# Two transformer blocks in float32: low parts of the feed-forwards' weight chunks by accumulating DMAs

## The chip, the cores and the metric

One core of a Trainium2 chip runs the whole program. The metric is the device time in microseconds of one execution; for the kernel before the median of three runs is given.

## What is computed

Two blocks of two layers each, on 512 tokens of width 1024, in float32. Every layer holds attention and mixing parts and feed-forwards, six in all:

```python
def swiglu(h, w_gate, w_up, w_down):
    return (jax.nn.silu(h @ w_gate) * (h @ w_up)) @ w_down

x = x + 0.5 * swiglu(rms_norm(x, ffn1_norm[l]), ffn1_w_gate[l], ffn1_w_up[l], ffn1_w_down[l])
...
x = x + 0.5 * swiglu(rms_norm(x, ffn2_norm[l]), ffn2_w_gate[l], ffn2_w_up[l], ffn2_w_down[l])
...
h = h + (jax.nn.silu(u @ w_gate[l]) * (u @ w_up[l])) @ w_down[l]
```

The weights are 1024 x 2816 (gate, up) and 2816 x 1024 (down). First block: feed-forward, mixing (convolutions and sparse attention), cross-attention, feed-forward. Second block: retention and differential attention, feed-forward. A norm ends each block.

## The kernel before

Tokens lie on the free axis: x is eight tiles of 128 x 512, and a product of the weights' chunk `c` (128 output channels, up to eight parts of 128 x 128) with the tokens fills one PSUM bank. A product in full precision is three products of rounded numbers: every operand is a high part, rounded to float32r, and a low part, the rest. `chunk` (L524) issues per part `w_hi * u_hi`, `w_hi * u_lo`, `w_lo * u_hi` (L542 to L544).

A weight chunk goes through a ring of four slots:

- SP's `load` (L431) waits until the low part of the chunk four back is made (`split`), then loads 512 KB into `raw`.
- ScalarE's `round_weights` (L1075) waits for the landing and for TensorE's end of the chunk four back (`tiles`), then writes `w_hi` (L1080).
- VectorE's `rest_of_weights` (L1534) waits for `rounded`, then writes `w_lo = raw - w_hi` (L1537) and counts `split`.
- TensorE's `chunk` waits for `split`.

So `step(p)` on ScalarE and `rest_of_weights(p)` on VectorE, called when chunk p is through TensorE, prepare chunk p + 4. A feed-forward has 68 chunks in three groups (`F_GROUPS`): gate and up chunks in turn (16, 16 and 12), after each eight down chunks of 8, 8 and 6 parts. The second gate and up of every four is mostly a *fast pair* (`fast_pair`, L588): seven half-size products in place of eight. It needs four sums of the pair's raw halves, which GpSimd makes one round ahead (`fast_sums`, L2279 to L2282, semaphore `s_made`); ScalarE rounds them (`sum_hi`, L1123) and VectorE splits them (`sum_lo`, L1601, `s_split`). There are 57 such pairs, seven in the first feed-forward and ten in the others.

At a feed-forward's end VectorE adds each down product to x (L1627), ScalarE and VectorE split the next input (`u_hi` L1084, `u_lo` L1541), and GpSimd's `squares` sums x squared (L2230, L2231). After the first chunk of the next stage (between the two blocks after the third) TensorE's `stat` needs the last square, VectorE scales it (L1577), GpSimd takes the power (L2257). Between the blocks GpSimd also sums a joint norm's squares (L2246).

All queues run in the order in which they are written; waits are on semaphores.

Of the kernel before, what the change touches and what calls it, by code (L numbers as in the profile page):

```python
# [36 lines left out]
KT = D // P  # L37
# [83 lines left out]
L2_AT = [2 * N_L1, 2 * N_L1 + N_L2]  # L121
assert all((n + c) % RING < 3 for n in L2_AT for c in D_V + R_V)

# [47 lines left out]
class At:  # L171


    def __init__(self, base, i=0):
        self.base, self.i = base, i
        self.slot, self.no, self.turn = base % RING, base + 4 * i, base // RING + i
# [5 lines left out]
def swapped(n, c):  # L182

    return c if (n - c % 2) % RING < 3 else c ^ 1

# [23 lines left out]
def two_blocks(nc, A, out):  # L209
    ctx = ExitStack()  # L210
    with ctx:
# [169 lines left out]
        split = sem("split")  # L381
        tiles = sem("tiles")
# [42 lines left out]

        block = ctx.enter_context(nc.Block())
# [94 lines left out]
        def _(pe):  # L521
            mm = nc.tensor.matmul

            def chunk(p, rhs_hi, rhs_lo, kn=KT, last=None, n=S, ks=None, order=None, to=None, after=None):  # L524


                order = order or range(kn)
                ks = ks or order
                if ks[0] == order[0]:
                    pe.wait_ge(split, p.no + RING + 1)  # L530
                    if after is None:
                        pe.wait_ge(taken, p.no + 1)
# [12 lines left out]
                if ks[-1] == order[-1]:  # L545
                    ins.then_inc(tiles, 1)
# [41 lines left out]
            def fast_pair(p, m, fast):  # L588
# [19 lines left out]
                pe.wait_ge(split, p.no + RING + 1)  # L608
# [9 lines left out]
                pe.wait_ge(split, p1.no + RING + 1)  # L618
# [66 lines left out]
            def values(p, hi, lo, blocks, outs, last, n=S, after=None):  # L685

                if blocks[0] == 0:
                    pe.wait_ge(split, p.no + RING + 2)
                    if after is None:
                        pe.wait_ge(taken, p.no + 2)  # L690
                if after is not None:
                    pe.wait_ge(taken, after + RING + 1)
                for t, o in zip(blocks, outs):
                    for k in range(KT):
                        u = slice(k * n + t * P, k * n + (t + 1) * P)
                        mm(o, hi[:, u], two_slots(w_hi, p, k), start=k == 0, stop=False)  # L696
                        mm(o, hi[:, u], two_slots(w_lo, p, k), start=False, stop=False)  # L697
                        ins = mm(o, lo[:, u], two_slots(w_hi, p, k), start=False, stop=k == KT - 1)  # L698
                    if t == last:
                        ins.then_inc(tiles, 2)  # L700
                    elif t == 1:
                        ins.then_inc(v_mm, 1)
# [368 lines left out]
        def _(act):  # L1071
# [3 lines left out]
            def round_weights(p, ahead=RING):  # L1075
# [14 lines left out]
            def step(p, more=True):  # L1090
                if more:
                    round_weights(p)
# [11 lines left out]
            def ffn(n, q, f, gain, more=True, joint=False):  # L1104
                for g, (f0, fn) in enumerate(F_GROUPS):
                    fast = quick(q, g)

                    def pair(p, f_at, h_at):

                        step(p)  # L1110
                        act.wait_ge(taken, p.no + RING + 1)
                        a(tanh_t, gate_t, ACT.Tanh, scale=0.5).then_inc(f_tanh, 1)
                        step(p.plus(1))
                        act.wait_ge(f_prod, F_TILES * f + f_at + 1)
                        a(tile(h_hi, h_at), gate_t, ACT.Copy).then_inc(f_rounded, 1)

                    def fast_pairs(p, m, f_at, h_at):
# [6 lines left out]
                        step(p)  # L1124
                        act.wait_ge(taken, p.no + RING + 1)
                        a(tanh_t, gate_t, ACT.Tanh, scale=0.5).then_inc(f_tanh, 1)
                        step(p.plus(1))
                        act.wait_ge(f_prod, F_TILES * f + f_at + 1)
                        a(tile(h_hi, h_at), gate_t, ACT.Copy).then_inc(f_rounded, 1)
                        step(q2)  # L1130
# [4 lines left out]
                        step(q3)  # L1135
# [3 lines left out]
                    if g == 0:  # L1139
                        if q:  # L1140
                            step(At(n))
                        step(At(n + 1))
# [25 lines left out]
                    def down(p, k, more):  # L1168
                        step(p, more)
# [8 lines left out]
                    if end and not more:  # L1178
                        for k in range(KT):
                            step(At(n + k), k < 4)  # L1180
# [59 lines left out]
            step(At(0))  # L1240
# [289 lines left out]
        def _(v):  # L1530
# [103 lines left out]
            def ffn(n, q, f, gain, factor, more=True):  # L1634

                for g, (f0, fn) in enumerate(F_GROUPS):
# [8 lines left out]
                    def up(p, f_at, h_at):  # L1645
# [6 lines left out]
                        rest_of_weights(p)  # L1652
# [13 lines left out]
                    def fast_up(p, m, f_at, h_at):  # L1666
# [11 lines left out]
                        rest_of_weights(p)  # L1678
# [3 lines left out]
                    if g == 0:  # L1682
                        rest_of_weights(At(n))
# [11 lines left out]
                        rest_of_weights(At(n + 2))  # L1695
# [4 lines left out]
                    with chain.loop(v, 1 if g == 0 else 0, fn // 2, 2 if fast is None else 5) as i:  # L1700
                        if fast is None:
                            for jj in range(2):
                                rest_of_weights(At(n + 2 * jj, i))
                                gate(At(n + 2 * jj, i), i * 2 + (f0 + jj))
                                up(At(n + 2 * jj + 1, i), i * 2 + (f0 + jj), i * 2 + jj)
                        else:
# [3 lines left out]
                            rest_of_weights(At(n, i))  # L1710
                            up(At(n + 1, i), i * 2 + f0, i * 2)
                            rest_of_weights(At(n + 2, i))
# [4 lines left out]
                    if end and not more:  # L1717
                        for k in range(KT):
                            residual(At(n + k), k, factor)
                            if k < 4:  # L1720
                                rest_of_weights(At(n + k))
# [9 lines left out]
                    with out_turns(v, after if end or not after else None) as turn:  # L1731
                        for i in (turn if (end or not after) and after in FAST else [turn]):
                            for j in range(4):
# [3 lines left out]
                                rest_of_weights(At(n + j, i))  # L1737
# [486 lines left out]
        def _(pool):  # L2224
# [11 lines left out]
            def squares(n, q):  # L2236
# [3 lines left out]
                if q == 8:  # L2240
                    chain.done(pool, nc.gpsimd.memset(j_sum, 0.0))
                with chain.loop(pool, 0, 2, 8 if q == 8 else 4) as i:
                    for j in range(4):
                        if q == 8:
                            pool.wait_ge(j_squared, i * 4 + (j + 1))
                            chain.done(pool, tt(j_sum, j_sum, tile(j_sq, i * 4 + j), ALU.add))  # L2246
# [12 lines left out]
            def fast_sums(n, q):  # L2259

                fast = FAST[q]
                pool.wait_ge(stat_diag, q + 1)

                def part(j):
                    return w_sum[:, j * HC:(j + 1) * HC]

                for g, (f0, fn) in enumerate(F_GROUPS):
                    if quick(q, g) is None:
                        n = n + 2 * fn + 8
                        continue  # L2270
                    with chain.loop(pool, 1 if g == 0 else 0, fn // 2, 2) as i:
                        p, m = At(n + 2, i), i + (FAST_PAIRS * fast + FAST_AT[g])
                        p1 = p.plus(1)
                        a11, a12 = raw[:, p.slot, 0:HC], raw[:, p.slot, HC:CH]
                        a21, a22 = raw[:, p1.slot, 0:HC], raw[:, p1.slot, HC:CH]
                        pool.wait_ge(s_split, m + 1)
                        pool.wait_ge(raw_in[p.slot], (p.turn + 1) * 16)
                        pool.wait_ge(raw_in[p1.slot], (p1.turn + 1) * 16)
                        tt(part(S3), a11, a21, ALU.add)  # L2279
                        chain.done(pool, tt(part(S1), a21, a22, ALU.add))  # L2280
                        chain.done(pool, tt(part(S2), part(S1), a11, ALU.add))
                        tt(part(S4), part(S2), a12, ALU.add).then_inc(s_made, 1)  # L2282
                    n = n + 2 * fn + 8
# [8 lines left out]
            for l in range(2):  # L2292
                L = L1_AT[l]
                turned = from_slot(L + O_OUT)
                fast_sums(L, 4 * l)
                squares(L + N_FFN - 8, 4 * l + 1)
# [39 lines left out]
                fast_sums(L + O_FFN2, 4 * l + 3)  # L2336
                squares(L + O_FFN2 + N_FFN - 8, 4 * l + 4)
                norm_inv(4 * l + 4)

            for l in range(2):  # L2340
# [16 lines left out]
                fast_sums(L + O2_FFN, 9 + 2 * l)  # L2357
                if l:
                    n = L + O2_FFN + N_FFN - 8
                    pool.wait_ge(taken, n + RING + 1)  # L2360
                    clear_sum()
                    for k in range(KT - 1):
                        pool.wait_ge(taken, n + k + RING + 1)
                        if k:
                            pool.wait_ge(sq_sum, 8 * 11 + k)
                        add_square(k)
                else:
                    squares(L + O2_FFN + N_FFN - 8, 10)
# [25 lines left out]
```

## Time and profile before

| | |
|---|---|
| median of 3 runs | 3486.97 us (3486.56 to 3487.17) |
| span of the profiled execution | 3487.4 us, 0.4 over that median |
| TensorE busy | 3439.7 us, 99% |
| VectorE | 2422.0 us, 69% |
| ScalarE | 1409.1 us, 40% |
| GpSimd | 958.4 us, 27% |
| loads of weights, share of the 16 DMA engines | 31.4% |

The profiled execution has no time of its own beside its span. A busy share is an average over stages with different limits; which engine a stage hangs on is read from its stretch and its waits. A matmul's busy time is modelled, and matmuls overlap, so TensorE's pace is read from the distance of their starts or of what waits for their ends.

### The profile page before, as it was taken

To read this page: it belongs to the slowest core of one execution; us is meant where nothing else is said; L and a number is where in the kernel's file an instruction comes from. 1 tells how busy PE (TensorE), PEld (TensorE's weight loads), DVE (VectorE), ACT (ScalarE), POOL (GpSimd) and SP (SyncE) were. 2 spreads that over 40 slices of the span, in tenths; PEclk is the share of its full clock that TensorE was granted. 3 is DMA by queue.
4 is the path that set the end of the run, shared out by engine and by line. 5 is a ranking of instruction groups with operands and counts; after the bars stand their busy time and mean duration, and the time that the engine had idled before them with its cause. 6 is when DMAs were issued, how large, how long until landed. Compare 5 with 4: busy or idle time off the path is not lost.

```text
span 3487.4 us, 51264 instructions
## 1 busy us (share of the span) xinstructions
PE 3439.7 (99%) x18454; PEld 2868.7 (82%) x18454; DVE 2422.0 (69%) x3375; ACT 1409.1 (40%) x2163; POOL 958.4 (27%) x631
## 2 busy tenths in 40 slices
PE   8999999999999999999999999999999999999998
PEld 7888786878888888878687888887888888888887
DVE  6667897558567967679755856765696585567755
ACT  4333365344334433336534433434443343443333
POOL 0112394123112511239412311230322130041213
PEclk9999999999999999999999999999999999999999
DMA  5332332323333333243232333331233332223331
GB/s 159 97 99 88 103 103 64 114 82 91 99 100 91 95 104 97 86 107 103 63 114 84 90 98 101 91 91 55 85 96 97 97 96 85 61 73 109 97 97 61
DMA packets 621280, 324.65 MB, mean 93 GB/s; under 512 B 13488, under 2 KB 616520, under 8 KB 621128
## 3 DMA queue, kind: packets, MB, share of 16 engines
q1 hardware_dynamic: 617096, 317.15, 31.4%
q10 hardware_dynamic: 4032, 5.51, 0.6%
q8 instruction: 91, 1.49, 0.2%
q14 instruction: 61, 0.50, 0.0%
HBM read 314.75 MB, written 2.10 MB: 91 GB/s over the span
## 4 chain that ended last, share of the span: by engine, by line
PE 84%; DVE 6%; issue 5%; ACT 2%; POOL 2%; DMA 0%; ACTq 0%; SPq 0%; DVEq 0%; POOLq 0%
PE bank L544 20%; PE bank L542 20%; PE bank L543 20%; PE bank L583 5%; PE bank L585 5%; PE bank L584 5%; POOL mem L2312 1%; PE bank L696 1%; PE bank L697 1%; PE bank L698 1%; DVE w_lo L1537 1%; PE bank L682 1%; PE bank L900 1%; PE bank L884 1%; PE bank L936 1%
## 5 line engine op out<-in xcount | busy, mean ns | idle before, releaser
L1080 ACT ACTIVATE w_hi<-raw 128x1024 fp32r<-128x1024 f32 x602 | 636.0, 1059 | 1201.6 <-PE bank L544 1184.9
L1537 DVE TENSOR_TENSOR w_lo<-raw,w_hi 128x1024 fp32r<-128x1024 f32 x602 | 839.8, 1397 | 202.9 <-ACT w_hi L1080 202.5
L542 PE MATMUL bank<-u_hi,w_hi 128*128 128x512 f32 x1920 | 763.4, 398 | 2.0 <-DVE mem L1546 1.5
L544 PE MATMUL bank<-u_hi,w_lo 128*128 128x512 f32 x1920 | 762.0, 397 | 0.0
L543 PE MATMUL bank<-u_lo,w_hi 128*128 128x512 f32 x1920 | 755.9, 394 | 0.0
L542 PE MATMUL bank<-h_hi,w_hi 128*128 128x512 f32 (+1 forms) x1568 | 606.7, 387 | 2.9 <-DVE h_lo L1541 2.2
L544 PE MATMUL bank<-h_hi,w_lo 128*128 128x512 f32 (+1 forms) x1568 | 608.5, 388 | 0.0
L543 PE MATMUL bank<-h_lo,w_hi 128*128 128x512 f32 (+1 forms) x1568 | 603.3, 385 | 0.0
L2279 POOL TENSOR_TENSOR mem<-raw 128x512 f32<-128x512 f32 x57 | 106.3, 1864 | 1334.4 <-DMA raw<-in_ffn_w_up 570.4
L542 PEld LDWEIGHTS bank<-u_hi,w_hi 128*128 128x128 f32 x1920 | 360.5, 188 | 92.0 <-issue 6.7
L544 PEld LDWEIGHTS bank<-u_hi,w_lo 128*128 128x128 f32 x1920 | 360.4, 188 | 87.1
L543 PEld LDWEIGHTS bank<-u_lo,w_hi 128*128 128x128 f32 x1920 | 360.7, 188 | 85.4
L1627 DVE SCALAR_TENSOR_TENSOR x<-bank,x 128x512 f32 (+1 forms) x192 | 132.4, 689 | 377.9 <-PE bank L544 377.8
L542 PEld LDWEIGHTS bank<-h_hi,w_hi 128*128 128x128 f32 x1568 | 294.4, 188 | 70.1 <-DVE h_lo L1541 4.8
L543 PEld LDWEIGHTS bank<-h_lo,w_hi 128*128 128x128 f32 x1568 | 294.7, 188 | 67.1 <-issue 0.5
L544 PEld LDWEIGHTS bank<-h_hi,w_lo 128*128 128x128 f32 x1568 | 294.5, 188 | 64.1
L2312 POOL TENSOR_TENSOR mem<-mem,spare 128x512 f32<-128x512 f32 x120 | 169.5, 1451 | 106.9 <-ACT spare L1302 106.5
L583 PE MATMUL bank<-t_hi,sum_hi 128*128 128x256 f32 x684 | 190.3, 278 | 3.5 <-DVE sum_lo L1601 3.5
L584 PE MATMUL bank<-t_lo,sum_hi 128*128 128x256 f32 x684 | 189.4, 277 | 0.0
L585 PE MATMUL bank<-t_hi,sum_lo 128*128 128x256 f32 x684 | 189.3, 277 | 0.0
L2231 POOL TENSOR_TENSOR mem<-mem 128x512 f32<-128x512 f32 x95 | 175.8, 1850 | 7.5
L2234 POOL MEMSET mem<- 128x512 f32 x12 | 6.3, 528 | 549.6 <-DVE x L1627 549.6
(300 smaller groups left out, 5863.1 us busy)
## 6 DMA issues: line engine op xcount, KB each, us to landing
raw<-in_w_in SPq DMA_DIRECT2D x96, 512.0 KB, 3.8
raw<-in_ffn_w_gate SPq DMA_DIRECT2D x88, 512.0 KB, 3.8
raw<-in_ffn_w_up SPq DMA_DIRECT2D x88, 512.0 KB, 3.8
raw<-in_ffn_w_down SPq DMA_DIRECT2D x64, 512.0 KB, 3.8
raw<-in_w_gate SPq DMA_DIRECT2D x44, 512.0 KB, 3.8
raw<-in_w_up SPq DMA_DIRECT2D x44, 512.0 KB, 3.8
raw<-in_w_out SPq DMA_DIRECT2D x32, 512.0 KB, 4.1
raw<-in_xa_wkv SPq DMA_DIRECT2D x32, 512.0 KB, 3.9
```

What stands on the lines that cost most here:

```text
L542: mm(o, w_hi[:, s, w], rhs_hi[:, r], start=k == order[0], stop=False)
L543: mm(o, w_hi[:, s, w], rhs_lo[:, r], start=False, stop=False)
L544: ins = mm(o, w_lo[:, s, w], rhs_hi[:, r], start=False, stop=k == order[-1])
L583: mm(o, wh, rh, start=k == 0, stop=False)
L584: mm(o, wh, rl, start=False, stop=False)
L585: ins = mm(o, wl, rh, start=False, stop=k == KT // 2 - 1)
L1080: a(w_hi[:, p.slot, :], raw[:, p.slot, :], ACT.Copy).then_inc(rounded, 1)
L1537: tt(w_lo[:, p.slot, :], raw[:, p.slot, :], f32(w_hi[:, p.slot, :]), ALU.subtract).then_inc(split, 1)
L1627: stt(tile(x, k), bank[p.slot][:, :], factor, tile(x, k), ALU.mult, ALU.add).then_inc(taken, 1)
L2231: tt(sumsq, sumsq, square, ALU.add).then_inc(sq_sum, 1)
L2279: tt(part(S3), a11, a21, ALU.add)
L2312: tt(conv[n % 2], conv[n % 2], tap_t[n % 4], ALU.add).then_inc(tap_added, 1)
```

## The change

In the feed-forwards VectorE no longer makes the chunks' low parts. ScalarE writes two roundings of the raw chunk, `w_hi` and, with a factor of -1, `w_lo`; then a DMA that GpSimd issues adds the raw chunk onto `w_lo`. Its landing is counted per slot (`low_in`), and TensorE and SP wait for that. GpSimd's program in a feed-forward is written out chunk by chunk, with the pairs' sums and the squares between the transfers. The descriptor memory for GpSimd's DMAs grows from 256 to 512 bytes a partition. The first four chunks of the program and all chunks of other stages stay with VectorE.

```diff
+FFN_AT = [0, O_FFN2, N_L1, N_L1 + O_FFN2, L2_AT[0] + O2_FFN, L2_AT[1] + O2_FFN]
+LOW = [c for n in FFN_AT for c in range(n + RING, n + N_FFN + RING) if c < N_ALL]
+def low_count(c):
+    return sum(b <= c and b % RING == c % RING for b in LOW)
...
+        def wait_split(eng, p):
+            if p.base + (0 if isinstance(p.i, int) else RING) in LOW:
+                eng.wait_ge(low_in[p.slot], (low_count(p.base) + p.i) * 16)
+            else:
+                eng.wait_ge(split, p.no + RING + 1 - sum(b < p.base for b in LOW))
...
-                sp_e.wait_ge(split, p.no + 1)
+                if p.base >= RING:
+                    wait_split(sp_e, p.plus(-RING))
...
-                    pe.wait_ge(split, p.no + RING + 1)
+                    wait_split(pe, p)
...
-                a(w_hi[:, p.slot, :], raw[:, p.slot, :], ACT.Copy).then_inc(rounded, 1)
+                ins = a(w_hi[:, p.slot, :], raw[:, p.slot, :], ACT.Copy)
+                if negated:
+                    ins = a(w_lo[:, p.slot, :], raw[:, p.slot, :], ACT.Copy, scale=-1.0)
+                ins.then_inc(rounded, 1)
...
-                        rest_of_weights(p)
                         v.wait_ge(f_rounded, F_TILES * f + f_at + 1)
...
+            def low(c):
+                pool.wait_ge(rounded, c + RING + 1)
+                nc.gpsimd.dma_start(w_lo[:, c % RING, :], raw[:, c % RING, :], accum_op=ALU.add).then_inc(low_in[c % RING], 16)
...
+            def first_sums(c, m):
+                a11, a12, a21, a22 = halves_of(c)
+                pool.wait_ge(s_split, m + 1)
+                for each in (c, c + 1):
+                    pool.wait_ge(raw_in[each % RING], (each // RING + 1) * 16)
+                tt(part(S3), a11, a21, ALU.add)
+                chain.done(pool, tt(part(S1), a21, a22, ALU.add))
+            def second_sums(c, m):
+                a11, a12, a21, a22 = halves_of(c)
+                chain.done(pool, tt(part(S2), part(S1), a11, ALU.add))
+                tt(part(S4), part(S2), a12, ALU.add).then_inc(s_made, 1)
+            def ffn(n, q, to=None):
...
+                        low(c)
...
+                            first_sums(*pairs[0])
+                        low(c + 1)
+                        if ahead:
+                            second_sums(*pairs.pop(0))
+                        low(c + 2)
+                        low(c + 3)
...
+                    for k in range(8):
+                        low(n + k)
+                        if k == 4 and pairs and pairs[0][0] == n + 10:
+                            first_sums(*pairs[0])
+                            second_sums(*pairs.pop(0))
...
+            def squares_and_low(n, q, to):
+                pool.wait_ge(taken, n + RING + 1)
+                clear_sum()
...
+                for k in range(KT):
+                    if not last or k < 4:
+                        low(n + k)
...
+                    add_square(k)
...
-    nc = bacc.Bacc("TRN2", target_bir_lowering=False, num_devices=1, dynamic_dma_scratch_size=256)
+    nc = bacc.Bacc("TRN2", target_bir_lowering=False, num_devices=1, dynamic_dma_scratch_size=512)
```

GpSimd in a round with a fast pair, first feed-forward; `mem` holds the sums. First before (the loop's body), then with the change.

```order
L2277 ISA [waits s_split]
L2279 TENSOR_TENSOR mem<-raw 128x512 [waits raw_in3,raw_in2]
L2280 TENSOR_TENSOR mem<-raw 128x512
L196 ISA
L2281 TENSOR_TENSOR mem<-mem,raw 128x512 [waits chain_p]
L196 REGISTER_ALU
L2282 TENSOR_TENSOR mem<-mem,raw 128x512 [waits chain_p]
```

```order
L2272 DMA w_lo<-raw 128x1024 [waits rounded] x3
L2288 TENSOR_TENSOR mem<-raw 128x512 [waits raw_in3,raw_in2,s_split]
L2289 TENSOR_TENSOR mem<-raw 128x512
L2272 DMA w_lo<-raw 128x1024 [waits rounded,chain_p]
L2294 TENSOR_TENSOR mem<-mem,raw 128x512
L2295 TENSOR_TENSOR mem<-mem,raw 128x512 [waits chain_p]
```

The four sums, alone before, now stand after one transfer and around another, and the next transfers stand behind them.

ScalarE at the start of the same round, before and with the change:

```order
L1122 ISA [waits s_made]
L1123 ACTIVATE sum_hi<-mem 128x2048 [waits w_mm]
L1077 ISA
L1079 REGISTER_ALU [waits raw_in0]
L1080 ACTIVATE w_hi<-raw 128x1024 [waits tiles]
L1125 REGISTER_ALU
L1126 ACTIVATE mem<-mem 128x512 [waits taken]
```

```order
L1147 ISA [waits s_made]
L1148 ACTIVATE sum_hi<-mem 128x2048 [waits w_mm]
L1099 ISA
L1101 REGISTER_ALU [waits raw_in0]
L1102 ACTIVATE w_hi<-raw 128x1024 [waits tiles]
L1104 ACTIVATE w_lo<-raw 128x1024
L1150 REGISTER_ALU
L1151 ACTIVATE mem<-mem 128x512 [waits taken]
```

The second rounding stands ahead of the tanh (L1126, now L1151).

GpSimd in the last down group of a feed-forward, before (`squares`, the first of four in the loop's body) and with the change:

```order
L2234 MEMSET mem 128x512 [waits taken]
L202 UNCONDITIONAL_BRANCH [waits chain_p]
L202 ISA
L2230 ISA [waits taken]
L2230 TENSOR_TENSOR mem<-x 128x512
L196 REGISTER_ALU
L2231 TENSOR_TENSOR mem<-mem 128x512 [waits chain_p]
```

```order
L2249 MEMSET mem 128x512 [waits taken]
L2272 DMA w_lo<-raw 128x1024 [waits rounded,chain_p]
L2245 TENSOR_TENSOR mem<-x 128x512 [waits taken]
L2246 TENSOR_TENSOR mem<-mem 128x512 [waits chain_p]
L2272 DMA w_lo<-raw 128x1024 [waits rounded]
L2245 TENSOR_TENSOR mem<-x 128x512 [waits sq_sum,taken]
```

Each chunk's square and sum now stand behind that chunk's transfer.

## Rows read from the trace of the kernel before

**Rows 1.** The page's first part: the span, and each engine's busy time, share and instructions.

```profile
span 3487.4 us, 51264 instructions
...
PE 3439.7 (99%) x18454; PEld 2868.7 (82%) x18454; DVE 2422.0 (69%) x3375; ACT 1409.1 (40%) x2163; POOL 958.4 (27%) x631
```

**Rows 2.** Busy time by stretch: the second feed-forward of layer 0.

```profile
core 0: us, PE busy (x) PEld busy (x) DVE busy (x) ACT busy (x) POOL busy (x), PEclk, DMA share, GB/s
805.00:1152.00 347.00, 345.77 (x1901) 296.89 (x1900) 256.53 (x284) 131.40 (x149) 90.93 (x55) 1.00 0.33 96
```

**Rows 3.** What TensorE waited for: us in total, times, longest.

```profile
PE bank L583 <- DVE sum_lo L1601: 3.5, 5, 0.9
...
PE bank L542 <- DVE h_lo L1541: 2.2, 6, 0.4
...
PE bank L542 <- DVE w_lo L1537: 0.7, 2, 0.4
```

**Rows 4.** Groups by line: busy, mean ns of one | idle before, releaser.

```profile
L1080 ACT ACTIVATE w_hi<-raw 128x1024 fp32r<-128x1024 f32 x602 | 636.0, 1059 | 1201.6 <-PE bank L544 1184.9
L1537 DVE TENSOR_TENSOR w_lo<-raw,w_hi 128x1024 fp32r<-128x1024 f32 x602 | 839.8, 1397 | 202.9 <-ACT w_hi L1080 202.5
```

**Rows 5.** Timeline (start, us) of ScalarE and SP's queue in a down group.

```profile
1043.90 1.06 ACT L1080 ACTIVATE w_hi<-raw 128x1024 fp32r<-128x1024 f32 x1 [4.54 <-PE bank L544]
1049.50 1.06 ACT L1080 ACTIVATE w_hi<-raw 128x1024 fp32r<-128x1024 f32 x1 [4.54 <-PE bank L544]
...
1046.25 0.37 SPq L436 DMA_DIRECT2D raw<-in_ffn_w_up  x1
```

**Rows 6.** Timeline of a round with a fast pair: ScalarE, then GpSimd.

```profile
1081.72 1.06 ACT L1080 ACTIVATE w_hi<-raw 128x1024 fp32r<-128x1024 f32 x1
...
1102.73 1.06 ACT L1080 ACTIVATE w_hi<-raw 128x1024 fp32r<-128x1024 f32 x1 [0.32 <-PE bank L544]
...
1084.86 2.03 POOL L2279 TENSOR_TENSOR mem<-raw 128x512 f32<-128x512 f32 x1 [14.32 <-DVE sum_lo L1601]
1086.85 1.29 POOL L2280 TENSOR_TENSOR mem<-raw 128x512 f32<-128x512 f32 x1
1088.22 1.63 POOL L2281 TENSOR_TENSOR mem<-mem,raw 128x512 f32<-128x512 f32 x1
1089.92 1.62 POOL L2282 TENSOR_TENSOR mem<-mem,raw 128x512 f32<-128x512 f32 x1
```

**Rows 7.** DMA queues (packets, MB, share); issues (count, KB each, us to landing).

```profile
q1 hardware_dynamic: 617096, 317.15, 31.4%
...
raw<-in_ffn_w_gate SPq DMA_DIRECT2D x88, 512.0 KB, 3.8
...
mem<-mem ACTq DMA_DIRECT2D x84, 64.0 KB, 2.1
...
mem<-in_mem SPq DMA_DIRECT2D x2, 1024.0 KB, 5.9
```

**Rows 8.** Timeline of the first feed-forward's end: ScalarE, then GpSimd.

```profile
372.50 1.06 ACT L1080 ACTIVATE w_hi<-raw 128x1024 fp32r<-128x1024 f32 x1 [2.41 <-PE bank L544]
...
376.70 1.06 ACT L1080 ACTIVATE w_hi<-raw 128x1024 fp32r<-128x1024 f32 x1 [1.94 <-PE bank L544]
...
378.90 2.16 POOL L2231 TENSOR_TENSOR mem<-mem 128x512 f32<-128x512 f32 x1
385.19 1.02 POOL L2257 TENSOR_TENSOR small<-small 128x4 f32<-128x4 f32 x1 [4.14 <-DVE small L1577]
```

**Rows 9.** Timeline of the end between the two blocks: GpSimd, then VectorE.

```profile
2259.27 1.53 POOL L2246 TENSOR_TENSOR mem<-mem 128x512 f32<-128x512 f32 x1 [0.62 <-ACT mem L1177]
...
2295.03 1.30 POOL L2231 TENSOR_TENSOR mem<-mem 128x512 f32<-128x512 f32 x1
...
2299.02 2.15 POOL L2231 TENSOR_TENSOR mem<-mem 128x512 f32<-128x512 f32 x1
...
2304.64 0.16 DVE L1577 TENSOR_SCALAR small<-bank 128x4 f32<-128x4 f32 x1 [4.62 <-PE bank L559]
```

More of the change, by code:

```diff
@@ L381, in two_blocks @@
         split = sem("split")
+        low_in = [sem(f"low_in{i}") for i in range(RING)]
         tiles = sem("tiles")
@@ L1073, in _, with round_weights @@
             chain = Chain(chain_a)
-            def round_weights(p, ahead=RING):
+            def round_weights(p, ahead=RING, negated=False):
                 act.wait_ge(raw_in[p.slot], (p.turn + (1 + ahead // 4)) * 16)
@@ L1088, in keep_rstd, with step @@
                 a(rstd[:, :], bank[7][:, :], ACT.Copy).then_inc(rstd_set, 1)
-            def step(p, more=True):
+            def step(p, more=True, negated=False):
                 if more:
-                    round_weights(p)
+                    round_weights(p, negated=negated)
             def round_summed(q, j):
@@ L1108, in pair @@
                     def pair(p, f_at, h_at):
-                        step(p)
+                        step(p, negated=True)
                         act.wait_ge(taken, p.no + RING + 1)
                         a(tanh_t, gate_t, ACT.Tanh, scale=0.5).then_inc(f_tanh, 1)
-                        step(p.plus(1))
+                        step(p.plus(1), negated=True)
                         act.wait_ge(f_prod, F_TILES * f + f_at + 1)
@@ L1134, in fast_pairs @@
                         a(tanh_t, gate_t, ACT.Tanh, scale=0.5).then_inc(f_tanh, 1)
-                        step(q3)
+                        step(q3, negated=True)
                         act.wait_ge(f_prod, F_TILES * f + f_at + 2)
@@ L1140, in ffn @@
                         if q:
-                            step(At(n))
-                        step(At(n + 1))
+                            step(At(n), negated=True)
+                        step(At(n + 1), negated=True)
                         if q:
@@ L1168, in down @@
                     def down(p, k, more):
-                        step(p, more)
+                        step(p, more, negated=True)
                         if end:
@@ L1179, in ffn @@
                         for k in range(KT):
-                            step(At(n + k), k < 4)
+                            step(At(n + k), k < 4, negated=True)
                             act.wait_ge(taken, n + k + RING + 1)
@@ L1239, in _ @@
             a(lam_s, lam_s, ACT.Exp).then_inc(lam_exp, 1)
-            step(At(0))
+            step(At(0), negated=True)
             keep_rstd(0)
@@ L2239, in squares @@
                 clear_sum()
-                if q == 8:
-                    chain.done(pool, nc.gpsimd.memset(j_sum, 0.0))
-                with chain.loop(pool, 0, 2, 8 if q == 8 else 4) as i:
+                with chain.loop(pool, 0, 2, 4) as i:
                     for j in range(4):
-                        if q == 8:
-                            pool.wait_ge(j_squared, i * 4 + (j + 1))
-                            chain.done(pool, tt(j_sum, j_sum, tile(j_sq, i * 4 + j), ALU.add))
                         pool.wait_ge(taken, At(n + j, i).no + RING + 1)
@@ L2257, in norm_inv @@
                 tt(inv, var, minus_half[:, 0:NQ], ALU.pow).then_inc(stat_inv, 1)
[L2259 to L2265, printed above, removed]
-                for g, (f0, fn) in enumerate(F_GROUPS):
-                    if quick(q, g) is None:
-                        n = n + 2 * fn + 8
-                        continue
[L2271 to L2283, printed above, removed]
@@ new lines, in second_sums @@
+            def second_sums(c, m):
[3 more added lines that the diff above has]
+            def ffn(n, q, to=None):
+                fast, at, turns = FAST.get(q), n, []
+                for g, (f0, fn) in enumerate(F_GROUPS):
+                    turns += [(g, i, at + 4 * i) for i in range(fn // 2)]
+                    at = at + 2 * fn + 8
+                pairs = [(c + 2, i + FAST_PAIRS * fast + FAST_AT[g]) for g, i, c in turns
+                         if quick(q, g) is not None and (g or i)] if fast is not None else []
+                if not q:
+                    low(n)
+                for g, (f0, fn) in enumerate(F_GROUPS):
+                    for i in range(fn // 2):
+                        c = n + 4 * i
+                        ahead = bool(pairs) and pairs[0][0] == c + 6
+                        if q or g or i:
+                            low(c)
+                        if ahead:
+                            if g == 0 and i == 0:
+                                pool.wait_ge(stat_diag, q + 1)
+                            first_sums(*pairs[0])
+                        low(c + 1)
+                        if ahead:
+                            second_sums(*pairs.pop(0))
+                        low(c + 2)
+                        low(c + 3)
+                    n = n + 2 * fn
+                    end = g == len(F_GROUPS) - 1
+                    if end and to is not None:
+                        squares_and_low(n, q, to)
+                        continue
+                    for k in range(8):
[3 more added lines that the diff above has]
+                            second_sums(*pairs.pop(0))
+                    n = n + 8
+                assert not pairs
@@ new lines, in squares_and_low @@
+            def squares_and_low(n, q, to):
+                clears = n + RING + 1
+                pool.wait_ge(taken, clears)
+                clear_sum()
+                if to == 8:
+                    chain.done(pool, nc.gpsimd.memset(j_sum, 0.0))
+                last = to == 12
+                for k in range(KT):
+                    if not last or k < 4:
+                        low(n + k)
+                    if last and k == KT - 1:
+                        continue
+                    if to == 8:
+                        pool.wait_ge(j_squared, k + 1)
+                        chain.done(pool, tt(j_sum, j_sum, tile(j_sq, k), ALU.add))
+                    pool.wait_ge(taken, n + k + RING + 1)
+                    if k:
+                        pool.wait_ge(sq_sum, 8 * (to - 1) + k)
+                    add_square(k)
@@ L2356, in _ @@
                 norm_inv(9 + 2 * l)
[L2357 to L2368, printed above, removed]
+                ffn(L + O2_FFN, 9 + 2 * l, 10 + 2 * l)
             norm_inv(12)
```

36 lines of the change are left out of this document (17 added, 19 removed).

## The prediction

> **What bounds the kernel now.** I read the summary first [rows 1]: TensorE (PE) is busy 3439.7 of 3487.4 us, VectorE (DVE) 69%, ScalarE (ACT) 40%, GpSimd (POOL) 27%. Then the stretches: in the second feed-forward of layer 0 TensorE is busy 345.77 of 347.00 us at the full granted clock, with the DMA engines at a third [rows 2]. So inside the feed-forwards, where all of the change lies, there is next to nothing to win on the bound engine. The list of what TensorE waits for says how little [rows 3]: 3.5 us for `sum_lo`, 2.2 for `h_lo`, 0.7 for `w_lo`, over the whole program: 6.4 us. VectorE's work on the low parts is large (602 x 1397 ns = 840 us [rows 4]) but lies beside TensorE.
>
> What the change can lose is read from the pace at which chunks must become ready. A chunk of eight parts lasts 5.60 us: ScalarE's rounding, which starts when TensorE ends a chunk, starts at 1043.90 and 1049.50 [rows 5]. A round of four chunks with a fast pair lasts 21.01 us (1081.72 to 1102.73) [rows 6], a chunk of the last down group 4.20 us (372.50 to 376.70) [rows 8].
>
> **The change, part by part.** There are 6 x 68 - 4 = 404 chunks whose low part moves.
>
> VectorE loses 404 subtractions, 404 x 1.40 = 564 us. They hid behind TensorE; of TensorE's waits at most the 6.4 us above go. I take -4.
>
> ScalarE gains 404 roundings with a factor of -1 over the same tile, at the 1.06 us of the first rounding [rows 4] 428 us. At 40% busy it has the room. A chunk's high and negated low part are done 0.1 + 2 x 1.06 = 2.2 us after TensorE frees the slot. At the end of a group the tile of h comes after ScalarE's second step, but VectorE no longer has its 1.2 us there. Priced at nothing; the cover is VectorE's time, and if it were gone the price would be about 1 us for each of 18 groups.
>
> GpSimd gains 404 transfers. No accumulating transfer is in the trace, so I bound its cycle C, from GpSimd's start on one to the landing that lets the next go. The nearest row is a weight load of the same 512 KB, 3.8 us to landing [rows 7]. Of this 31.4% x 3487.4 us / 605 loads' worth of bytes = 1.8 us is packet time, so some 2.0 us do not grow with size. An addition reads two operands. Lower end: one pass, 3.8 us, with an issue as short as SP's 0.37 [rows 5]: 4.2. Upper end: 1024 KB take 5.9 us [rows 7], and an issue of a whole small GpSimd instruction, 1.02 us [rows 8]: 6.9. I take 5.1, nearer the lower end, since both sides lie in SBUF, where 64 KB land in 2.1 us [rows 7]. I also take it that one is in flight at a time: the descriptor memory is 512 bytes a partition. The page Collectives: The Full Stack of the Trainium skill (The bandwidth ceiling) says that a DMA reduction "needs two source reads", at about half the rate of a copy; no run here shows it yet.
>
> Latency alone is covered: landed at 2.2 + 5.1 = 7.3 us, needed three chunks later, 21.0 - 5.6 = 15.4. About 8 us of slack. SP's load of the slot's next chunk waits for the landing instead of VectorE, and every later load stands behind it in SP's queue; 3.8 us later it has landed, long before its rounding 21 us on. The waits themselves, on one count per slot, and the folded turn numbers I price at nothing: TensorE's queue takes them beside its matmuls, as it does now. What counts is whether the serial line of transfers and sums keeps pace:
>
> - Fast round. GpSimd's four sums for the next pair now stand between transfers. The first two need the pair's second raw chunk, whose load now waits for the landing of the transfer just before them. So each round holds, in series, load 3.8 + first two sums 3.3 (2.03 + 1.29 [rows 6]) + three transfers 3C = 7.1 + 15.3 = 22.4 us against 21.0. That is 1.4 late per round; it breaks even at C = 4.6. There are eight such rounds in a feed-forward (five in the first): +11.2. The other two sums (3.3 us) run during a flight.
> - First and second down group: 8 x 5.1 us, and of one pair's sums (6.6 us) the 2.5 that a flight does not cover, 43.3 against 44.8: -1.5 each, -3.0.
> - Last down group: 40.8 against 8 x 4.2 = 33.6: +7.2.
>
> So the line is 15.4 us late at the end of a feed-forward. Part of this shows as TensorE waiting for low parts (what exceeds 8 us), the rest a chunk later: the squares of x stand behind the transfers on GpSimd, and the statistic needs the last of them. Before, it had no room either: the last square ends at 378.90 + 2.16 = 381.1 [rows 8], and the statistic follows one chunk after 376.6, at some 382.3. So I price the whole lateness: 16 us after three feed-forwards (15.4, and half a microsecond for the last transfer's issue ahead of the last square), 12 after the first with its three rounds fewer.
>
> Between the two blocks the statistic comes three chunks after the end, 11.2 us later, but GpSimd also adds the joint squares: it went from 2259.27 to 2301.17 for eight chunks, 5.2 us each [rows 9], and with some 0.8 of issue 6.0, against 4.2. VectorE took the statistic at 2304.64. Lateness 8 + 8 x 1.8 = 22.4, less the 11.2 and the 1 us or so to spare: +10. The last feed-forward ends with four transfers: 11.2 - 3.0 + 4 x 0.9 = 11.8, less the slack of 8: +4.
>
> Sum: 12 + 3 x 16 + 10 + 4 - 4 = +70. The span of 3487.4 is 0.4 over the median of the runs, 3486.97, so I forecast **3557 us**.
>
> **Rivals.**
>
> 1. *Hidden.* If C is at most 4.6, or several transfers may be in flight, every round keeps pace. For it: the engines' third of use leaves room, and 4.2 is my lower end. Left are the ends: ScalarE's second step ends 2.2 us after the last chunk, at 378.9, the last transfer's issue at 379.9, two GpSimd operations of 2.8 to 3.3 us follow, so that the statistic waits 0.5 to 3 us at four places, up to 5 between the blocks, against -4 to -6: 3481 to 3500, likeliest 3490. The page DMA: Bandwidth & Descriptors of the Trainium skill (Anatomy of one DMA) gives 2.0 us + bytes/436e3 for a DMA from GpSimd: with two reads C would be 4.4 (estimate), just this case; no GpSimd DMA is in this trace. Chance 0.27.
> 2. *The transfers become the pace.* If C is 6.0, a round holds 7.1 + 18 = 25.1, +4.1 x 8 = 33; three rounds ahead of the down groups 24 - 21 = 3 each, 9; two down groups 48 + 1.6 - 44.8, 10; the last 14: 66 us per feed-forward, some 380 in all: 3867. At 6.9 it is nearer 620 in all. For it: 1024 KB take 5.9 us here, and loads share the engines. Chance 0.25, from 3700 up.
> 3. *Faster.* One mechanism: VectorE's relief where TensorE waits for VectorE, at the first fast pair (`sum_lo`, 3.5 us over five) and at the last h tiles (2.2 over six), with 0.7 for `w_lo` and about a microsecond of refilling: -7.3, 3480. It decides only if C is below about 4.5, and if GpSimd's squares, 2.16 us beside VectorE's subtraction where 1.30 is the shortest [rows 9], speed up enough to pay for the issues. Chance 0.05.
> 4. *Not what it says:* the low parts that VectorE keeps (attention and mixing, 602 - 404 = 198) are untouched, and the waits in the code name the right chunks; I see no way for the transfers to be left out.
>
> **How the numbers follow.** The forecast (C between 4.6 and 5.6 or so, 3495 to 3700) has 0.43, the hidden case 0.27, the slow case 0.25, faster 0.05. About 0.2% (7 us) is what a measurement of this kernel can tell from no change. Of the hidden case 0.20 lies within that and 0.07 above; so faster 0.05, same 0.20, slower 0.75. The likeliest case's own range is 3495 to 3700. The range leaves out the faster end and C over 6.0 (0.15): 3482 to 3870.
>
> **What would show it.** Right: TensorE's waits name DMA of `w_lo` from `raw`, mostly late in the groups and in the last down group; GpSimd starts transfers about 5 us apart with nothing else between; the wait before the statistic grows to several microseconds; VectorE some 560 us less busy, ScalarE 430 more, DMA use up by a third to two thirds of what it was. Wrong: transfers that land in under 4.2 us or overlap (rival 1), or over 5.6 us (rival 2); or TensorE waiting for ScalarE's roundings, which I priced at nothing.

## The result and the profile after

The changed kernel takes 4039.72 us (4038.29 to 4041.11, 4 runs), the kernel before 3486.76 in the same comparison: a ratio of 1.1584, interval 1.157 to 1.1598, or 553 us more. The forecast was 3557, the range 3482 to 3870. The direction was forecast, the size was not.

The page of the changed kernel: the span, the engines, and the DMA queues (packets, MB, share of 16 engines); q0 holds the new transfers, q1 the loads.

```profile
span 4039.1 us, 50532 instructions
...
PE 3596.7 (89%) x18454; PEld 2928.2 (72%) x18454; DVE 1912.6 (47%) x2971; ACT 1791.8 (44%) x2567; POOL 1229.0 (30%) x1035
...
q1 hardware_dynamic: 617096, 317.15, 27.7%
q0 software_dynamic: 58176, 211.84, 26.7%
```

Against [rows 1], VectorE is 509 us less busy, ScalarE 383 more, and TensorE, with the same 18454 matmuls, 157 more (instructions that overlap count once there; the low parts' subtractions alone fell by 559 us, from 839.8 to 280.9). What TensorE waited for (us in total, times, longest):

```profile
PE bank L563 <- DMA w_lo<-raw: 306.5, 195, 4.9
PE bank L575 <- POOL mem L2246: 41.8, 4, 11.2
PE bank L604 <- DMA w_lo<-raw: 20.1, 30, 1.6
```

The first and third are waits for transferred low parts, 326.6 us where [rows 3] had 6.4 us for VectorE; the second is the statistic at four feed-forwards' ends. With TensorE's 157 us they make 525 of the 553. Since the order of TensorE's matmuls is the same in both traces, the start of each can be compared with its twin before: the difference grows by 94, 95, 89, 93, 99 and 80 us in the six feed-forwards, and stays within a few microseconds between them.

The second feed-forward of layer 0, longer now, by stretch; columns as in [rows 2]:

```profile
895.00:1345.00 450.00, 378.66 (x1943) 311.35 (x1942) 177.42 (x228) 199.56 (x221) 140.06 (x125) 0.96 0.67 155
```

No engine is full: the DMA engines are at two thirds, VectorE and ScalarE under a half, TensorE waits. What is full is seen in GpSimd's timeline (start, us; in brackets the idle time before and what ended it), here with SP's queue below it, in rounds with a fast pair:

```profile
1060.25 0.88 POOL L2272 DMA_DIRECT2D w_lo<-raw  x1 [5.56 <-ACT w_lo L1104]
1064.48 1.34 POOL L2288 TENSOR_TENSOR mem<-raw 128x512 f32<-128x512 f32 x1 [3.35 <-DMA raw<-in_ffn_w_up]
...
1067.91 0.89 POOL L2272 DMA_DIRECT2D w_lo<-raw  x1 [0.41 <-POOL mem L2289]
...
1073.05 0.90 POOL L2272 DMA_DIRECT2D w_lo<-raw  x1 [1.54 <-issue]
1079.39 0.87 POOL L2272 DMA_DIRECT2D w_lo<-raw  x1 [5.45 <-issue]
...
1066.62 0.37 SPq L457 DMA_DIRECT2D raw<-in_ffn_w_gate  x1
1072.75 0.37 SPq L457 DMA_DIRECT2D raw<-in_ffn_w_up  x1
1079.13 0.37 SPq L457 DMA_DIRECT2D raw<-in_ffn_w_gate  x1
```

At 1073.05 and 1079.39 GpSimd issues a transfer 0.3 us after SP has issued a load (1072.75, 1079.13): the landing of the transfer before (1072.73, 1079.07) lets both go. The bracket at 1060.25 names ScalarE, but its rounding for that chunk had ended at 1047.72, and the landing before came at 1059.94. In all but 10 of the 394 gaps of the table below ScalarE's rounding was done before that landing. From 1073.05 to 1079.39 a cycle, from one issue to the next, lasts 6.34 us. The one at 1067.91 stood behind two sums, so that SP's load (1066.62) was 1.3 us ahead of it: 5.14 us. At the program's end SP has no load left, and the cycles are 4.86 and 4.85:

```profile
4002.05 0.88 POOL L2272 DMA_DIRECT2D w_lo<-raw  x1 [3.10 <-ACT w_lo L1104]
...
4006.91 0.91 POOL L2272 DMA_DIRECT2D w_lo<-raw  x1 [1.54 <-issue]
...
4011.76 0.89 POOL L2272 DMA_DIRECT2D w_lo<-raw  x1 [1.50 <-issue]
```

Of the 404 transfers 394 have a next issue within 9.5 us. Sorted by the packet time of the loads that started between the one issue and the next:

| load packets beside it, us per engine | transfers | cycle | first packet after the issue by | packets from first to last | from there to the next issue |
|---|---|---|---|---|---|
| up to 0.5 | 18 | 4.85 | 1.46 | 2.77 | 0.64 |
| 1.0 to 1.5 | 53 | 6.28 | 2.29 | 3.29 | 0.62 |
| 1.5 to 2.0 | 286 | 6.60 | 2.68 | 3.22 | 0.63 |
| over 2.0 | 21 | 6.69 | 2.69 | 3.23 | 0.64 |

(medians in us, each column by itself; over 2.0 means up to 3.0, 4 more lie between 0.5 and 1.0 and 12 over 3.0). Beside a whole load the first packet comes 1.2 us later and the packets take 0.45 longer. The shortest distance of two issues in the whole trace is 4.82 us: never are two in flight.

### The profile page after: what moved, and what is told of

The parts are those of the page before. It is cut to its first block, busy times and chain, and to the rows that moved or that the text cites. A ratio compares the mean times of both kernels' runs of the same rounds, so it can differ in the third digit from the quotient of the medians.

```text
span 4039.1 us, 50532 instructions
## 1 busy us (share of the span) xinstructions
PE 3596.7 (89%) x18454; PEld 2928.2 (72%) x18454; DVE 1912.6 (47%) x2971; ACT 1791.8 (44%) x2567; POOL 1229.0 (30%) x1035
## 3 DMA queue, kind: packets, MB, share of 16 engines
q0 software_dynamic: 58176, 211.84, 26.7%
## 4 chain that ended last, share of the span: by engine, by line
PE 39%; DMA 24%; issue 18%; POOL 11%; ACT 5%; DVE 3%; ACTq 0%; POOLq 0%; SPq 0%; DVEq 0%
DMA w_lo<-raw 17%; PE bank L563 10%; PE bank L565 10%; PE bank L564 10%; DMA raw<-in_ffn_w_up 2%; ACT w_lo L1104 2%; POOL mem L2246 2%; POOL w_lo L2272 2%; POOL mem L2245 2%; POOL mem L2289 1%; ACT w_hi L1102 1%; PE bank L718 1%; POOL mem L2295 1%; DMA raw<-in_w_up 1%; POOL mem L2294 1%
## 5 line engine op out<-in xcount | busy, mean ns | idle before, releaser
L563 PE MATMUL bank<-u_hi,w_hi 128*128 128x512 f32 x1920 | 793.8, 413 | 156.6 <-DMA w_lo<-raw 144.0
L2272 POOL DMA_DIRECT2D w_lo<-raw x404 | 356.4, 882 | 1679.3 <-issue 1100.3
L563 PE MATMUL bank<-h_hi,w_hi 128*128 128x512 f32 (+1 forms) x1568 | 636.9, 406 | 174.8 <-DMA w_lo<-raw 162.5
L565 PE MATMUL bank<-u_hi,w_lo 128*128 128x512 f32 x1920 | 779.9, 406 | 0.0
L564 PE MATMUL bank<-u_lo,w_hi 128*128 128x512 f32 x1920 | 777.0, 405 | 0.0
L564 PE MATMUL bank<-h_lo,w_hi 128*128 128x512 f32 (+1 forms) x1568 | 619.5, 395 | 0.0
L564 PEld LDWEIGHTS bank<-u_lo,w_hi 128*128 128x128 f32 x1920 | 374.1, 195 | 86.0
L1104 ACT ACTIVATE w_lo<-raw 128x1024 fp32r<-128x1024 f32 x404 | 421.4, 1043 | 0.0
L1562 DVE TENSOR_TENSOR w_lo<-raw,w_hi 128x1024 fp32r<-128x1024 f32 x198 | 280.9, 1425 | 150.7 <-ACT w_hi L1102 150.6
L1566 DVE SCALAR_TENSOR_TENSOR u_lo<-x,par,u_hi (+1 forms) x88 | 140.8, 1600 | 79.4 <-ACT u_hi L1109 79.4
```

Of the source, the lines that this page charges most:

```text
L1104: ins = a(w_lo[:, p.slot, :], raw[:, p.slot, :], ACT.Copy, scale=-1.0)
L1562: tt(w_lo[:, p.slot, :], raw[:, p.slot, :], f32(w_hi[:, p.slot, :]), ALU.subtract).then_inc(split, 1)
L1566: stt(dst_lo, src, scale, f32(dst_hi), ALU.mult, ALU.subtract).then_inc(e, 1)
L2272: nc.gpsimd.dma_start(w_lo[:, c % RING, :], raw[:, c % RING, :], accum_op=ALU.add).then_inc(low_in[c % RING], 16)
```

## Experiments

My theory from these rows (A): additions run one at a time, and each meets the load that the landing before it let go, so that its cycle is 6.6 us in place of 4.85; four of them don't fit into the 21.0 us of a round, and the line of transfers sets the pace. Rivals: the DMA engines or GpSimd limit the rate whatever is in flight (B); ScalarE's second rounding makes the low parts late (C); load, sums and transfers stand in series, as the prediction had it.

**Two in flight.**

```diff
-dynamic_dma_scratch_size=512
+dynamic_dma_scratch_size=640
```

> Only the descriptor memory grows from 512 to 640 bytes a partition, so that two transfers may be in flight. Theory A (one transfer in flight at a time, and each meets the load that the landing before it released, so that its cycle is 6.5 to 7 us in place of the 4.85 it has alone): the engines' packets for one addition and one load take 2.64 + 1.8 = 4.4 us, under the 5.25 us a chunk of TensorE, so the pace is no longer the transfers'; 3490 to 3580 us. Theory B (the DMA engines or GpSimd's own issue limit the rate, however many are in flight): over 3950. Theory C (ScalarE's second rounding makes the low parts late): over 3950 too.

Measured: 3510.34 us, ratio 1.0069 (1.0051 to 1.0088). One number gives back 529 of the 553 us. The page, what TensorE waited for, and GpSimd's timeline of the second feed-forward's first fast rounds:

```profile
PE 3443.2 (98%) x18454; PEld 2867.0 (82%) x18454; DVE 1996.6 (57%) x2971; ACT 1780.6 (51%) x2567; POOL 1213.7 (35%) x1035
...
q0 software_dynamic: 58176, 211.84, 33.1%
...
PE bank L563 <- DMA w_lo<-raw: 16.6, 13, 3.1
...
834.47 0.86 POOL L2272 DMA_DIRECT2D w_lo<-raw  x1 [3.29 <-ACT w_lo L1104]
841.79 1.34 POOL L2288 TENSOR_TENSOR mem<-raw 128x512 f32<-128x512 f32 x1 [6.47 <-DMA raw<-in_ffn_w_up]
...
844.98 0.87 POOL L2272 DMA_DIRECT2D w_lo<-raw  x1 [0.41 <-POOL mem L2289]
...
848.81 1.77 POOL L2272 DMA_DIRECT2D w_lo<-raw  x2
```

Two issues stand back to back at 848.81 ("x2"), 0.9 us apart. TensorE is at 98% again. B and C fall as the main cause: the same bytes, the same roundings, the same sums. What is left, 23 us, comes by the comparison of starts nearly all in the feed-forwards' first four rounds (1 to 5 us each); 3 us more come near 200 us in the first feed-forward, and 2.5 between the two blocks.

**Half of every load; half of every addition.**

```diff
-load(At(n + j, i), W[...], l, 0, KT, ...)
+load(At(n + j, i), W[...], l, 0, KT // 2, ...)
...
-load(At(n + j, i), W[down], l, f0, fn, ...)
+load(At(n + j, i), W[down], l, f0, fn // 2, ...)
```

> Leaves out: half of every weight chunk's load in the feed-forwards (256 KB in place of 512), the other half of the buffer keeps old data. Theory A: the load's share of the transfer's cycle falls by some 0.9 us, to 5.6 to 6.0; 3700 to 3860 us. If loads don't matter to the transfer's cycle (its latency is its own): within 40 of 4040.

```diff
-nc.gpsimd.dma_start(w_lo[:, c % RING, :], raw[:, c % RING, :], accum_op=ALU.add)
+nc.gpsimd.dma_start(w_lo[:, c % RING, 0:HC], raw[:, c % RING, 0:HC], accum_op=ALU.add)
```

> Leaves out: half of every accumulating transfer's columns (256 KB in place of 512), with the same number of descriptors. Theory A: 1.3 us less packet time per transfer, cycle 5.2 to 5.6; 3580 to 3760 us. If the time of a transfer doesn't grow with its bytes: within 40 of 4040.

Measured: 3633.73 us (ratio 1.042, 1.0399 to 1.044) with half loads, 3576.05 (1.0254, 1.0234 to 1.0275) with half additions, each under its band, by 66 and by 4 us. The cycle beside a half load is 5.34 (334 transfers); half an addition takes 3.6 alone and 5.29 beside a whole load (224). So loads matter to an addition's cycle: taking half of the load away gains 1.26 us of it, taking half of the addition away 1.31. That a transfer's time is its own, or doesn't grow with its bytes, is refuted. But the load's packet time is not simply added: a whole load (1.86 us) lengthens the cycle by 1.75 us, half a load (0.90) by 0.49 only. Why half costs so little stays open.

**ScalarE's part alone.**

```diff
-a(w_hi[:, p.slot, :], raw[:, p.slot, :], ACT.Copy).then_inc(rounded, 1)
+ins = a(w_hi[:, p.slot, :], raw[:, p.slot, :], ACT.Copy)
+if negated:
+    ins = a(w_lo[:, p.slot, :], raw[:, p.slot, :], ACT.Copy, scale=-1.0)
+ins.then_inc(rounded, 1)
```

> The kernel before with ScalarE's second rounding alone: it writes the negated rounding to the low part, and VectorE's subtraction then writes over it. Theory A: ScalarE is not the cause; 3485 to 3500 us, VectorE's subtraction 1.06 us later. Theory C (ScalarE's second rounding is what makes low parts late): over 3550.

Measured: 3501.3 us, ratio 1.0042 (1.0027 to 1.0056): at the band's edge, and not nothing. TensorE's waits of this run:

```profile
PE bank L583 <- DVE sum_lo L1604: 9.4, 5, 1.9
...
PE bank L542 <- DVE u_lo L1544: 3.8, 5, 0.9
```

`sum_lo` has 9.4 us where [rows 3] has 3.5. Where both engines do their parts one after the other, the second rounding shows, by the comparison of starts mostly in the feed-forwards' first rounds. C is a matter of 14 us, not of 553.

**Fewer additions on the same line.** Chunks of two (three) of the four ring slots go by addition, VectorE subtracts for the others.

```diff
+VEC = [c for c in LOW if c % RING in (1, 3)]
...
+if in_vec(p):
+    tt(w_lo[:, p.slot, :], raw[:, p.slot, :], f32(w_hi[:, p.slot, :]), ALU.subtract).then_inc(low_in[p.slot], 16)
...
+if c + RING in VEC:
+    return
```

> One transfer in flight as in the change, but only chunks of two of the four ring slots go by transfer (ScalarE's second rounding too); VectorE subtracts for the others. Theory A (a line of transfers that can't keep the pace of 21 us per four chunks): two transfers of 6.5 us and the sums fit into a round, so that all but the starts is hidden; 3488 to 3515 us. If every transfer costs its share wherever it stands: half of the +553, 3720 to 3800.

Measured: 3489.54 us, ratio 1.0006 (0.9997 to 1.0015), no change. Half of the additions cost nothing that can be measured, so an addition has no price of its own as long as the line keeps pace.

> As the run with two of the four ring slots by transfer, one in flight, now three of four. Theory A (a line against TensorE's 21 us per four chunks): three transfers of 6.5 us and more, one of them 4.85 behind the sums, fill 18 to 20 us of 21, so that the pace still holds in most stretches; 3490 to 3540 us. If each transfer costs in proportion from some count on, half of what the fourth slot brings: 3600 to 3900.

Measured: 3580.22 us, ratio 1.0269 (1.0251 to 1.0286), above the band. By the comparison of starts some 65 of the trace's 85 us come in the last down groups and at the statistic behind them (16 of 29 in the first feed-forward): three cycles of 6.6 are 19.8 us against 4 x 4.2 = 16.8 there. I had set the line against a fast round and forgotten the short chunks. So the price goes 0, 0.027, 0.158 for two, three and four slots: a threshold, as theory A has it, with a lower one in the last down group.

**Without the sums.**

```diff
-tt(part(S3), a11, a21, ALU.add)
-chain.done(pool, tt(part(S1), a21, a22, ALU.add))
...
-chain.done(pool, tt(part(S2), part(S1), a11, ALU.add))
-tt(part(S4), part(S2), a12, ALU.add).then_inc(s_made, 1)
...
+nc.gpsimd.memset(w_sum[:, 0:1], 0.0).then_inc(s_made, 1)
```

> Leaves out: GpSimd's four sums of every fast pair (about 5.2 us of GpSimd per pair; the sums stay zero). Theory A: at a cycle of 6.5 and more beside a load, a transfer that follows the sums has no load beside it and takes 4.85, so the sums cost little; 4000 to 4045 us. If load, sums and three transfers stand in series as the prediction had it (load and two sums 7.1 us of each round): the sums' 3.3 us go 57 times, about 3850.

Measured: 4017.92 us, ratio 1.1522 (1.1501 to 1.1543): 22 us less than with the sums. In the 40 fast rounds that follow another, the four cycles of the changed kernel have medians of 7.53 (the load that the sums wait for, and two sums), 5.41, 6.49 and 6.52 us, a round 25.84; without the sums they are 6.42, 6.44, 6.38 and 6.55, a round 25.93. So load and two sums do stand in the line, as the prediction had it, but the transfer behind them takes 1 us less: at this cycle a round lasts four cycles with or without the sums.

**A copy in place of the addition, then one copy at a time.**

```diff
-nc.gpsimd.dma_start(w_lo[...], raw[...], accum_op=ALU.add).then_inc(low_in[c % RING], 16)
+nc.gpsimd.dma_start(w_lo[...], raw[...]).then_inc(low_in[c % RING], 16)
```

> Leaves out: the addition; the transfer copies the raw chunk onto the low part, with the same bytes written. If the addition doubles the transfer's packet time by its second read (2.64 us against 1.3 for a copy): cycle 5.2 beside a load and 3.6 alone, as with half of the columns; 3560 to 3610 us. If adding costs no more than copying: within 40 of 4040.

Measured: 3485.57 us, ratio 0.999 (0.9979 to 1.0). I had expected a shorter transfer, still one at a time. Its queue and issues:

```profile
q0 software_dynamic: 58176, 211.84, 17.4%
...
45.87 0.53 POOL L2272 DMA_DIRECT2D w_lo<-raw  x1 [5.41 <-ACT w_lo L1104]
48.40 0.54 POOL L2272 DMA_DIRECT2D w_lo<-raw  x1 [2.01 <-ACT w_lo L1104]
...
w_lo<-raw POOLq DMA_DIRECT2D x404, 512.0 KB, 3.3
```

At 45.87 and 48.40 two issues are 2.53 us apart where one takes 3.3 to land (median; the first of these landed at 48.72): two copies were in flight in the same 512 bytes, where two additions never are. In the whole trace 45 copies were issued before the one ahead had landed. The run had changed two things, the addition and the number in flight. So the next one holds the copies apart:

```diff
+at = LOW.index(c + RING)
+if at:
+    pool.wait_ge(low_in[LOW[at - 1] % RING], low_count(LOW[at - 1]) * 16)
```

> Leaves out: the addition, as in the run with the plain copy; and GpSimd waits for the landing of the transfer before it issues the next, so that again one is in flight. It tells what the copy saved: theory A1 (one in flight is what costs, and the addition's second read lengthens each): cycle 3.6 alone and about 5.2 beside a load, as with half of the addition's columns; 3540 to 3600 us. A2 (the addition's length alone costs, and one at a time is enough for copies): 3480 to 3500.

Measured: 3685.84 us, ratio 1.0568 (1.055 to 1.0586), above both bands. A copy alone has a cycle of 3.3, beside a load 5.6 (216 transfers; first packet after 2.94, as late as the addition's 2.68). So of the 553 us, 200 come from one at a time even with plain copies, and the other 354 from the addition's length, as long as one is in flight; with two in flight the whole change costs 23. The packets' time is 17.4% x 3487.5 / 404 = 1.50 us for a copy, and 26.7% x 4039.1 / 404 = 2.67 us for an addition of as many bytes.

**What is left with two in flight.** Two guesses. First: VectorE makes the low parts of each feed-forward's first round (not in the first), since ScalarE is busiest there.

```diff
+VEC = [n + RING + j for n in FFN_AT[1:] for j in range(4)]
```

> Two transfers in flight (640 bytes), and in the last five feed-forwards VectorE makes the low parts of the chunks that are prepared in the first round of four, where ScalarE's queue is long; ScalarE leaves the second rounding out there. Theory: what is left with two in flight (+23 us) is lost at the feed-forwards' starts, 3 to 5 us each, because the second rounding and the transfer stand behind ScalarE's other work there; 3488 to 3500 us, of which the unchanged first feed-forward has 6 to 7. If the rest is spread over all chunks instead: 3505 to 3515.

Measured: 3507.75 us, ratio 1.0059 (1.0045 to 1.0072): within noise of the run with two in flight, and in the band of the rival. But the loss is not spread over all chunks either: by the comparison of starts it moved a round later and did not go; this guess falls. Second, from the timeline above: at 834.47 a transfer is issued, then GpSimd stands until 841.79 for the load that the first sums need, and the next transfer (844.98) stands behind the sums, though ScalarE's roundings for it were done at 836.5.

```diff
 low(c)
-if ahead: first_sums(*pairs[0])
 low(c + 1)
-if ahead: second_sums(*pairs.pop(0))
+if ahead: first_sums(*pairs[0]); second_sums(*pairs.pop(0))
 low(c + 2)
```

> Two in flight (640 bytes), and GpSimd issues the round's second transfer ahead of the first two sums in place of behind them. Theory: what is left with two in flight is the first sums' wait for the load of the pair's second chunk, with a ready transfer queued behind it in the first fast rounds of each feed-forward; 3488 to 3500 us. If the longer flights themselves are what is late there: 3505 to 3515.

Measured: 3490.23 us, ratio 1.0007 (0.9997 to 1.0017): the kernel before and this one can't be told apart. The same place in its trace, and what TensorE waited for:

```profile
831.85 0.86 POOL L2272 DMA_DIRECT2D w_lo<-raw  x1 [3.29 <-ACT w_lo L1104]
834.68 0.86 POOL L2272 DMA_DIRECT2D w_lo<-raw  x1 [1.96 <-ACT w_lo L1104]
839.24 1.29 POOL L2288 TENSOR_TENSOR mem<-raw 128x512 f32<-128x512 f32 x1 [3.71 <-DMA raw<-in_ffn_w_up]
...
PE bank L563 <- DMA w_lo<-raw: 2.5, 3, 0.9
```

The second transfer (834.68) now goes while the load is under way, and the wait for low parts falls from 16.6 to 2.5 us. With a bigger descriptor memory and that order the idea costs nothing, and gains nothing either. None of the runs beats the kernel before by more than its interval.

## Why the prediction was wrong

- **What bounds the kernel**: right. Nothing was to be won: with the transfers out of the way (the run with two in flight and the new order, the run with copies) the time is that of before within 0.1%, with VectorE at 56% and 55%.
- **VectorE's and ScalarE's terms**: right in size. 404 second roundings took 421.4 us (428 forecast), and the subtractions fell by 559 (564). "Priced at nothing" holds only while VectorE does not subtract behind them; with its subtraction they cost 14 us, where the prediction had about 18 for that case.
- **C, the cycle of a transfer: the step that failed.** I sized a transfer as if it ran alone and took 5.1 us. Alone it takes 4.85. But it is hardly ever alone: the landing that lets the next addition go also lets SP's load go, and both run on the same 16 engines. The prediction had both halves of this in front of it, 1.8 us of packet time per load [rows 7] and the sentence that SP's load waits for the landing, and priced what the load does to the transfer at nothing. 4.85 + 1.8 = 6.65; measured 6.60. That this sum comes out so well holds for the whole load alone, as the run with half loads shows. The bound of 6.9 did hold the measured C, but the range of the forecast left out C over 6.0.
- **The second read**: the Trainium skill, page Collectives: The Full Stack (The bandwidth ceiling), says of ReduceScatter that its add needs two source reads, and that it comes to about half of the rate of AllGather, which copies. The traces agree: 2.67 us of packets for an addition, 1.50 for a copy, 1.8 times as much. By the Trainium skill's page DMA: Bandwidth & Descriptors (Anatomy of one DMA) C was estimated at 4.4 with two reads; measured 4.85 alone, and 6.60 beside a load, which that sum for one transfer leaves out.
- **One in flight**: right, and decisive. I took it from the size of the descriptor memory; the issues' shortest distance (4.82 us against 0.58 with 640 bytes) shows it. It was in part luck: the same 512 bytes held two copies, so the size alone did not say it.
- **The working of the sum**: it held, given C, within some 5%. Rival 2's terms, taken at C = 6.6, make a round of 26.9 us and give a feed-forward 47 + 16 + 18 + 19 = 100 us (eight fast rounds, three rounds ahead of the down groups, two down groups, the last); the first has three fast rounds less (83), the last four transfers less (91). Measured: 94, 95, 89, 93, 99 and 80, together 550 against some 576. The parts agree less well than the sum: a fast round measured 25.84. Rival 2's "nearer 620" for C = 6.9 does not come out of its own terms, which give some 680.
- **The ends**: the statistic waits 41.8 us at four places, where the prediction had it; but most of the loss lies before them, spread over the feed-forwards; and where the line is only a little too slow (three slots), the last down group and that wait are most of the loss.
- **The chances**: rival 2 had 0.25 and "loads share the engines" among its reasons. It should have been the forecast.

What stays open is the share of TensorE's clock. It was granted 0.965 on average, 0.994 before: 284 us at the lower level, half of the full clock, in 59 stretches, where the kernel before had 44 in 7, and TensorE was 157 us longer busy. These stretches come with the waits and are gone when the waits go (37 us with two in flight). It can hardly be a large part by itself: from the last packet of one transfer to the issue of the next lie 0.63 us as a rule, and in 394 gaps together only 82 us more than that, so that the line of transfers hardly ever waited for TensorE. No run holds the clock and leaves the waits.

## What to carry to other kernels

When the landing of one transfer lets another start, price them together: here a whole load brought an addition's cycle from 4.85 to 6.60 us, and the cycle measured alone was only its lower bound. Ask of every transfer that is issued from a small descriptor memory how many may be in flight, and compare the pace that this allows with the consumer's pace in the shortest stretch, not in the mean one. And where the bound engine is 99% busy, as here, moving work off another engine can do little more than tie.

## What the hardware showed that I had not expected

- The same 512 bytes of descriptor memory held two copies in flight (two issues 2.53 us apart, the first landing 2.85 after its issue) but one addition (never under 4.82 us); 640 bytes held two additions. An addition's issue also took longer on GpSimd, 0.88 us against 0.54.
- A load issued 0.3 us ahead of a transfer delays its first packet from 1.46 to 2.68 us after the issue, and stretches its packets by only 0.45: most of the load goes first (1.54 of its 1.86 us of packets begin ahead of the addition's first).
- With pauses of a few microseconds per chunk TensorE's granted clock fell to the lower level in 59 stretches, 284 us in all, though it was busy 89% of the span.
